# Half of the channel tiles projected inside the scan loop, and a first norm apart from the parameter vectors

## The reference

```python
proj = h @ w_in                                # z 2048, x 2048, B 512, C 512, dt 32
xpad = concat([conv_state, xbc])
conv = depthwise_conv(xpad, conv_w, width=4)
new_conv_state = xpad[:, -3:]
xbc = silu(conv + conv_b)
y, h_last = ssd_scan(xs, dt, a, bm, cm, ssm_state)   # chunks of 128 tokens; sample rows: one step
y = y + xs * d_skip
y = y * silu(z)
y = y * rsqrt(mean(y * y) + EPS) * norm_g
return y @ w_out, new_conv_state, h_last
```

## Time and profile before

| what | us |
|---|---|
| median of 3 runs (1757.2 to 1758.83) | 1758.48 |
| the profiled execution, by the device | 1757.71 |
| its span in the trace | 1756.0 |
| first norm and vectors, to the first projection matmul | 0 to 20.89 |
| 24 channel tiles, to the first z tile | 20.89 to 122.54 |
| scan loop, to the last offset decay | to 255.14 |

### The profile page before, as it was taken

One profiled execution on the slowest core, in us unless ns is written; L12 is line 12 of the kernel. 1 busy time (PEld: TensorE's weight loads), 2 busy tenths in 40 slices (PEclk: granted clock), 3 DMA queues, 4 the chain that ended last, 5 costly groups with the idle time before them and its releaser, 6 DMA issues.

```text
span 1756.0 us, 21537 instructions
## 1 busy us (share of the span) xinstructions
PE 1657.3 (94%) x8029; PEld 964.8 (55%) x8029; DVE 642.8 (37%) x1382; ACT 451.8 (26%) x1166; POOL 133.3 (8%) x280
## 2 busy tenths in 40 slices
PE   7999879899999999998999999989899999999997
PEld 5887666734443444343877878766644443444342
DVE  3658992322221222123023354654422221222123
ACT  3439861211111111112143142232301111111112
POOL 1122420100000000002001101320000000000000
PEclk9999989899999999999999999999899999999999
DMA  9456762379999999999344736775279999999994
GB/s 329 145 181 201 209 242 96 112 321 416 428 429 428 428 428 429 428 428 398 123 142 158 275 112 247 220 229 230 96 298 417 428 430 429 428 428 429 429 427 196
DMA packets 101362, 537.72 MB, mean 306 GB/s; under 512 B 7964, under 2 KB 32740, under 8 KB 76690
## 3 DMA queue, kind: packets, MB, share of 16 engines
q1 hardware_dynamic: 85520, 485.18, 68.1%
q0 software_dynamic: 15360, 51.30, 9.1%
q10 hardware_dynamic: 418, 0.39, 0.1%
HBM read 520.61 MB, written 16.42 MB: 306 GB/s over the span
## 4 chain that ended last, share of the span: by engine, by line
PE 65%; DMA 17%; DVE 11%; ACT 4%; issue 2%; POOL 0%; SPq 0%; ACTq 0%; DVEq 0%
PE bank L847 21%; DMA ring<-in_moe_w_gate_up 13%; PE bank L1170 8%; PE bank L859 8%; PE bank L833 6%; PE bank L1085 5%; PE bank L752 4%; PE bank L853 4%; PE bank L1128 3%; DMA arena<-sample_queries 2%; PE bank L1364 2%; ACT arena L1668 1%; DVE arena L2086 1%; DVE arena L2168 1%; PE bank L1208 1%
## 5 line engine op out<-in xcount | busy, mean ns | idle before, releaser
L847 PE MATMUL bank<-ring,arena 128*64 128x512 f32 x2048 | 449.5, 594 | 20.5 <-DMA ring<-in_moe_w_gate_up 19.4
L847 PEld LDWEIGHTS bank<-ring,arena 128*64 128x64 f32 x2048 | 153.9, 137 | 309.5 <-issue 309.5
L1170 PE MATMUL bank<-hT,ring 128*128 128x264 f32 x1152 | 274.1, 395 | 0.0
L1170 PEld LDWEIGHTS bank<-hT,ring 128*128 128x128 f32 x1152 | 218.6, 193 | 45.1 <-issue 9.1
L859 PE MATMUL bank<-ring,arena 128*64 128x512 f32 x1024 | 226.8, 595 | 0.0
L1947 DVE TENSOR_TENSOR arena<-arena,bank 128x512 f32<-128x512 f32 x32 | 34.3, 1070 | 414.1 <-ACT arena L1450 414.1
L859 PEld LDWEIGHTS bank<-ring,arena 128*64 128x64 f32 x1024 | 70.7, 137 | 134.9 <-issue 134.9
L853 PE MATMUL bank<-arena 128*128 128x512 f32 x272 | 134.9, 618 | 1.7 <-ACT arena L1460 1.6
L752 PE MATMUL bank<-ident,arena 128*128 128x128 f32 (+6 forms) x609 | 103.9, 284 | 30.0 <-DMA arena<-in_ssm_d 10.3
L1450 ACT ACTIVATE arena<-bank 128x512 f32<-128x512 f32 x32 | 19.1, 597 | 414.4 <-PE bank L847 414.4
L752 PEld LDWEIGHTS bank<-ident,arena 128*128 128x128 f32 (+6 forms) x609 | 72.9, 144 | 91.9 <-issue 45.8
(11 more groups left out here) (325 smaller groups left out, 1538.4 us busy)
## 6 DMA issues: line engine op xcount, KB each, us to landing
ring<-in_moe_w_gate_up SPq DMA_DIRECT2D x128, 2048.0 KB, 16.3
ring<-in_moe_w_down SPq DMA_DIRECT2D x64, 2048.0 KB, 12.9
ring<-in_attn_qkv SPq DMA_DIRECT2D x18, 2048.0 KB, 9.0
ring<-in_ssm_in_proj SPq DMA_DIRECT2D x10, 2048.0 KB, 15.2
out<-arena POOLq DMA_DIRECT2D x24, 512.0 KB, 4.2
arena<-in_cache_kv_w POOLq DMA_DIRECT2D x20, 512.0 KB, 8.0
ring<-in_ssm_out_proj SPq DMA_DIRECT2D x4, 2048.0 KB, 10.2
arena<-in_state_ssm SPq DMA_DIRECT2D x16, 512.0 KB, 4.6
```

Source lines behind the costliest of these rows:

```text
L847: mm = pe.matmul(bank[j][e * SLOTS:(e + 1) * SLOTS, :], Xg[:, 4 * half + k, 2 * h + e, :], weights(2 * half + e)[:, k, j * DE:(j + 1) * DE ...
L1170: mm = pe.matmul(bank[i % 2][:, 0:T], wv[:, k, (i % 4) * P:(i % 4 + 1) * P], hT[:, k, :], start=(k == 0), stop=(k == DT - 1))
```

## The change

Twelve of the 24 channel tiles (B, C and the first four of x) are projected ahead of the loop, and tile 12+t in step t of the loop, for t from 0 to 11, with its raw copy, its convolution and its silu, which is done for two tiles at a time beside the silu of two z tiles. It goes through bank 3, so the decay rows have bank 2 alone: `cs_rows(t)` waits for the decays of step t-1 instead of t-2. Raw buffers go from 8 to 4, state buffers from 3 to 2, outer-product buffers from 2 to 1, so the outer products of step t wait for the state update of step t-1. The input weights' chunks alternate between x and z, and the states' loads are spread between them on SyncE's queue. Four of the six sets of column transposes move into the output projection. On VectorE `finish` comes ahead of `scores`, and the sample rows' steps are made for two steps at a time. In the first norm, the vectors' transposes move behind the first pass of transposes and VectorE's copies behind its scaled rows; three of the small transfers move to SyncE's queue ahead of weight chunk 0, three others on ScalarE's queue behind the load of its function table. The names that change their line are the same functions.

```diff
-RAWS = 8
-STATES = 3
+RAWS = 4
+LEAD = 4
+PRE = 2 * SG + LEAD
+STATES = 2
...
+        st_in = m(STATES, NS, N)
+        outer = m(NS, N)
...
-        in_cols = [2 * DI, 2 * DI + 512] + [DI + 512 * i for i in range(4)] + [512 * i for i in range(4)]
+        in_cols = [2 * DI, 2 * DI + 512] + [c + 512 * i for i in range(4) for c in (DI, 0)]
```

On SyncE:

```diff
+                for t in {8: (0, 1), 9: (2,), 10: (3,), 11: (4, 5, 6), 12: (7,), 13: (8, 9, 10)}.get(n, ()):
+                    states_in(t)
```

On GpSimd:

```diff
+            for t in range(XT_TILES + 1):
+                u, g = t - 1, (t - 1) // TPG
+                if PRE + t + 1 < CT:
+                    old_columns(PRE + t + 1)
...
+                    pool.wait_ge(s_So, u + 1)
+                    pool.dma_start(ssm_p[0, 0, 2 * u:2 * u + 2].rearrange("h p n -> (h p) n"),
+                                   hout[:, u % 2, :]).then_inc(s_Sst[u % 2], 16)
+                if t >= 2:
+                    squares(t - 2)
+                if t >= 1:
+                    pool.wait_ge(s_h, u + 1)
+                    pool.dma_start(ssm_s[0, :, 2 * u:2 * u + 2].rearrange("b h p n -> (h p) b n"),
+                                   st_in[:, u % STATES, :, :]).then_inc(s_hst[u % STATES], 16)
+                if PRE + t < CT:
+                    new_columns(PRE + t)
```

On TensorE:

```diff
             def norm(k, xn):
+                first = DT if k else DT - 1
                 pe.wait_ge(n_xn, XN_BASE[k] + 1)
-                for d in range(DT):
+                for d in range(first):
                     transpose(bank[d][:, 0:P], xn[:, 0, d * P:(d + 1) * P])
+                if k == 0:
+                    vectors()
...
             def cs_rows(t):
-                if t == 1:
-                    pe.wait_ge(s_dcv, 2)
-                if t >= 2:
-                    pe.wait_ge(s_dec, t - 1)
+                if t:
+                    pe.wait_ge(s_dec, t)
...
             for t in range(XT_TILES):
                 g = t // TPG
+                if PRE + t < CT:
+                    conv_tile(PRE + t)
+                elif t + 1 < XT_TILES:
+                    z_tile(t + 1)
                 if t + 1 < XT_TILES:
                     cs_rows(t + 1)
                     x_rows(t + 1)
                 if t % TPG == 1 and g + 1 < SG:
                     cb_products(g + 1)
-                if t + 1 < XT_TILES:
+                if PRE + t < CT:
                     z_tile(t + 1)
                 scan_products(t)
...
+                if 1 <= d <= 4:
+                    new_columns(d + 1)
```

On ScalarE:

```diff
-                if t >= 2:
-                    act.wait_ge(s_h, t - 1)
+                act.wait_ge(s_tkv, 6 + t // 2)
+                if t >= 1:
+                    act.wait_ge(s_h, t)
...
+            for t in range(XT_TILES + 1):
+                if t >= 1:
+                    decay_and_state(t - 1)
+                if t == XT_TILES:
+                    break
+                decays(t)
+                if t % 2:
+                    for j in (PRE + t - 2, PRE + t - 1):
+                        if j < CT:
+                            conv_silu(j)
+                    z_silu(t)
+                if PRE + t < CT:
+                    raw_copy(PRE + t)
+                if t >= 2:
+                    square(t - 2)
+                    gain(t - 2)
+                outer_products(t)
+                if t + 1 < XT_TILES:
+                    z_copy(t + 1)
```

On VectorE:

```diff
+            def sample_steps(p):
+                v.wait_ge(s_cx, 2 * (2 * SG + 2 * p + 2))
+                ts = slice(2 * p, 2 * p + 2)
+                v.tensor_tensor(dtx[:, ts, :], dtx[:, ts, :], conv_out[:, ts, TP:T], ALU.mult).then_inc(s_tkv, 1)
...
             for t in range(XT_TILES + 1):
                 g = t // TPG
+                if t >= 1:
+                    finish(t - 1)
                 if t < XT_TILES:
                     scores(t)
-                if t >= 1:
-                    finish(t - 1)
-                if t + 1 < XT_TILES:
-                    x_steps(t + 1)
                 if t % TPG == 2 and g + 1 < SG:
                     masked_cb(g + 1)
                 if t >= 1:
                     decode(t - 1)
+                if t + 1 < XT_TILES:
+                    x_steps(t + 1)
+                if PRE + t < CT:
+                    convolve(PRE + t)
+                if t >= 1:
                     gate(t - 1)
+                if t % 2 and t + 1 < XT_TILES:
+                    sample_steps((t + 1) // 2)
```

263 lines of the change are left out of this document (136 added, 127 removed).

## The result

The changed kernel takes **1739.88 us** (median of 4 runs, 1739.69 to 1740.75) against 1758.65 (4 runs, 1757.2 to 1760.75): 18.8 us less, a ratio of 0.9893 with a 95% interval of 0.9876 to 0.991. Its profiled execution took 1740.03 us, 1738.3 of them in the trace.

The account below looks back on a forecast made before the run. TensorE was taken to bound the projection ahead of the loop, VectorE the scan loop. Terms -2.3 (start), -5.5 (loop), +1.8 (column transposes) gave -6.0: 1751.7 us profiled, 1752.5 as a median, range 1743 to 1760.

Parts of the forecast that it names:

- Start: First norm up to the first projection matmul: root no longer waits for the parameter vectors; gain 1.7 to 2.9, 2.3 taken.
- Shorter prefix: Projection ahead of the loop: 12 tiles (43.0 us), column transposes (1.3), products and decay rows (1.56) leave; first z tile at 76.7.
- Twelve fuller steps: Loop steps with a moved tile: VectorE bounds at 10.93 us a step, TensorE 10.35, ScalarE 8.2; 11 steps take 120.2.
- the sum's price: GpSimd's running sum of squares stretches VectorE's work with two SBUF operands, 0.85 to 0 us a step; 0.8 taken.
- sums cost nothing: Rival, chance 0.20: sums of squares over state updates are free, TensorE bounds at 10.35 us a step; 1743.0.
- Last four steps: Loop steps without tiles: single outer buffer and ScalarE's order close a ring, 9.25 us each, 37.0 in all; before 7.90 each.
- Loop in sum: End of the scan loop: last offset decay at 249.6 us, before 255.14, so 5.5 gained; same output projection behind it.
- Column transposes: Four sets moved into the output projection, where TensorE bounds: 4 x 0.43, 1.8 us lost.
- All that comes behind ... moves the end one for one: Behind the first layer's state-space part, weights stream into a ring waiting for TensorE; gains before 256 us reach the end unchanged.
- The clock in the loop: Rival, chance 0.13: TensorE's clock falls in the loop; at mean 0.88 the step is 11.76 us, total 1761.6, slower than before.
- Level engines and queues: Rival, chance 0.17: three level engines with in-order queues lose 0.55 us in each of 11 steps, 6 in all; 1758.
- State loads and chunks: Loop with two state buffers for three: store (up to 5.7 us) and load (4.6) fit in 18.9, covered even with a 2 MB chunk between.

Follow-up runs that it names:

- the second profiles of both kernels: Both kernels run again unchanged: the changed kernel 1739.3 us (0.9901), the kernel before 1756.68 us (1.0002).
- the sum behind the store: Changed kernel with GpSimd's running sum of squares moved back behind the issue of the state store: 1735.49 us, 0.9863 to the kernel before.
- the tiny sum: Changed kernel with GpSimd's sum of squares taken over 4 of its 264 columns only, at its place: 1733.19 us, 0.986 to the kernel before.
- the single silu: Changed kernel with the silu of the convolution's tiles done for each step instead of for pairs: 1738.6 us, 0.9886 to the kernel before.
- the best version: Changed kernel with sum of squares behind state store, root's table load early, logits' clearing and router's gain ahead of variance: 1729.7 and 1730.99 us.

## Why the prediction was wrong

Its sum gave 6.0 us; the profiled executions differ by 17.7. Three terms hold nearly all of the miss: the fuller steps (4.2 us), the event that ends the loop (3.9) and what lies behind the first layer (3.3). The first was a matter of size, the second of mechanism, the third was put at nothing.

**Start: right in mechanism, too small.** Forecast 2.3, in this pair 1.9, by the runs about 3. "First matmul at 18 to 19 us" held.

**Shorter prefix: right, 1.3 short.** 44.5 instead of 45.9 us left it; 1.1 of the difference is the first tile, 6.39 us for 5.33. By the second profiles of both kernels it is 45.4.

**First steps of the loop.** From the first z tile to the first offset decay it took 15.00 us. The prediction used 15.7 (92.4 less 76.7), though the terms that it lists for this stretch add up to 15.3: 0.4 of the 0.7 is a slip of addition.

**Twelve fuller steps: right in mechanism, 4.2 too high.** The 11 steps took 115.95 us, not 120.2, or 10.54 each. Work on VectorE was 10.03, not 10.13; the sum's price 0.57, not the 0.8 I took; the first two steps were TensorE's, at 9.9 on average. That VectorE bounds, that the sum is a price on the state updates, and that ScalarE has slack, all held: the sum behind the store and the tiny sum both give the price back. The rival "sums cost nothing" fell by this, though its 1743.0 lies nearer: it too had its end at the wrong event.

**Last four steps: right in sum, and partly by luck**, 36.4 for 37.0. From scores to scores they take 8.83, 9.47 and 8.42, 0.3 less than the 9.25 on average, since the sum costs the updates 0.00 to 0.90 there; the last offset decay then comes later than that by what stands ahead of it.

**Loop in sum: the step whose mechanism failed.** "249.6 for the last offset decay, before 255.14 ... Behind it TensorE runs the same output projection." The last offset decay was a fair mark for the old loop, where it stood 1.89 us behind the scan products. In the new one ScalarE does outer products, a silu of z and two table loads first, and it stands 5.81 behind, while TensorE has gone on to the projection with the first 14 of its 16 input tiles and needs the last two only some 14 us later. Moving it moved nothing. **3.9 us** of the gain were missed by following a mark instead of what the next stage waits for.

**Column transposes: hidden under other terms.** Forecast 1.8 lost. From the scan products of step 15 to the first expert matmul it is 1.25 longer (92.10 for 90.85), by the second profiles of both kernels 3.6 (91.86 for 88.25). That holds the root's table load (6.50 for 5.28 us from the sum to the router) too, which I did not see; the clock differs from one execution to the next there, so neither pair gives the transposes' price alone.

**Not in the sum: 3.3 us behind the first expert matmul.** "All that comes behind ... moves the end one for one" was wrong by this much. 2.0 are in the attention. One window of TensorE there, before, then after:

```profile
1021.00:1031.00 10.00, 10.00 (x57) 0.85 0.01 2
```

```profile
1007.00:1017.00 10.00, 9.60 (x71) 1.00 0.01 2
```

Before has such a slice in both of its profiles (0.85 and 0.87); the changed kernel has none in either of its two, but six of the other versions have it. The part takes 373.8 to 374.9 us with it and 371.3 to 373.1 without. What decides it stays open. The last 1.4 are the first profile of before alone, whose clock was 0.92 over that stretch; its second profile lacks them.

In sum: start -0.4, prefix -1.3, z tile to first offset decay +0.7, 11 steps +4.2, last four +0.6, the mark +3.9, projection +0.6, behind it +3.3: 11.6 of the 11.7 us.

**Rivals.** The clock in the loop was 1.00 up to 210 us and fell only in the last steps, 0.77 and 0.79, where VectorE bounds. Level engines and queues cost nothing in the steps with a tile: VectorE has no wait from 125 to 205 us, and the single silu shows ScalarE's slack. State loads and chunks were covered: neither TensorE nor VectorE waits for a transfer between 76 and 256 us. What the single outer-product buffer and the two state buffers cost was not tried by itself.

**Not priced at all** was VectorE's order, worth 9.6 us with the sum where it is. A sum of durations does not see an order. In the old order the 11 steps take 120.7 us, where I forecast 120.2: the right number for another kernel.

## What to carry to other kernels

Forecast the event that the next stage waits for, on the engine that waits, and not the one that was last before: a reordering changes which is last. Where a loop closes a ring between engines, write the ring down with every instruction that the new order puts into it, since two swapped lines were worth half the change here. And where a wait is added ahead of an instruction that may need a table load, look at which of the two gets it.

## What the runs showed of the hardware

**VectorE and GpSimd on SBUF.** A sum of 0.75 us costs the state updates 0.91 if it starts 0.33 us into them, and 0.49 if it starts at 1.04 and takes 0.95 itself. Over a reduction it costs nothing. The Trainium skill (SBUF — State Buffer, section "SBUF: two separate sides") has an exclusive lock, with the first one keeping the ports for its whole instruction. The trace agrees that they exclude each other: in each set that meets a sum one single update is held, until 0.15 us behind the sum's end (1247 ns and 829 ns for 340), and the seven others are as fast as alone. It does not agree on who keeps the ports. In the first case the held update's row begins 0.33 us ahead of the sum's, in the second 0.27 behind it; in step 15 the sum is held to 1.34 us behind updates that had begun. Whether a row begins when its access to SBUF does, no run shows.

**A table load can carry a wait.** With one wait ahead of the root it ran 6 us early; with two it took the first and stood in the chain for 1.28 us; with the second wait moved away it ran early again, 3.4 us ahead of the root. The Trainium skill (ScalarE: Activation LUTs, section "What ACT_TABLE_LOAD costs") gives 2.66 us for a switch, a drain included. Here taking one off the chain gave TensorE 1.34 us back, and the load's row is followed by the root after 0.01 us: no drain shows.

**The clock behind a stall.** TensorE stood idle at the root for 5.00 us in the changed kernel, 3.66 with the root's load early and 2.93 with the router's gain ahead too. Behind it the granted clock fell to 0.5 to 0.7 in one of the next windows of 4 us, so for part of them to the lower of the two levels (1.2 GHz for 2.4), also after 2.93 us (0.63, then 0.51). In both profiles of the best version it stayed 1.00 after 2.93 us, and 2 us were won. That version differs from the one whose clock fell by the sum's place alone, so by what TensorE did ahead of the stall; what in it keeps the clock stays open.

**Half rate under a listed clock of 1.00.** In the first projection tile the counts begin 0.44 us apart and then 0.22, in windows where the profile lists 1.00. The trace's own record of clock changes has its first entry, to 1.00, at 24.20 us, and the last slow count begins at 23.98, the next at 24.32. In all 17 profiles the change of rate lies within 0.15 us of this first entry, which comes anywhere from 20.7 to 26.9 us. So ahead of the first entry the listed 1.00 is no reading, and the length of the first tile goes by when the clock rises in that execution.
